# The last modulation of a hybrid trunk layer: from TensorE strips in the state-space stage to GpSimd products in the RWKV stage

## What is computed

```
mod = (silu(cond) @ w_ada + b_ada).reshape(6, 2048)   # cond: 2048 values, w_ada: 2048 x 12288
shift_m, scale_m, gate_m, shift_f, scale_f, gate_f = mod
h = rms_norm(x) * (1 + scale_m) + shift_m
proj = h @ w_in
mixed = concat(ssd_mixer(proj[..., :2592]), rwkv7_mixer(proj[..., 2592:])) @ w_out
x = x + gate_m * mixed
h = rms_norm(x) * (1 + scale_f) + shift_f
x = x + gate_f * expert_choice_ffn(h)                 # 16 experts, 400 MB of weights
y = rms_norm(x)
```

## Time and profile before

| | |
|---|---|
| median of 3 runs | 2311.43 us (2304.68 to 2314.29) |
| the profiled execution | 2312.1 us |
| its span, first to last instruction | 2310.1 us |
| mean granted TensorE clock | 0.978 |
| state-space pairs, from the first of their strips | 197 to 460 us |
| RWKV stage | 461.8 to 1182 us |
| output projection | 1187 to about 1300 us |
| experts | to the end |

### The profile page before, as it was taken

How to read it: one execution, slowest core, us unless ns; L and a number is a source line. 1 busy time by engine, 2 the same in 40 slices (tenths; PEclk the granted TensorE clock), 3 DMA queues, 4 the chain that set the end, 5 groups by cost and what they waited for, 6 DMA issues and landing times. The chain is left out here.

```text
span 2310.1 us, 38354 instructions
## 1 busy us (share of the span) xinstructions
PE 2124.0 (92%) x16411; PEld 1067.5 (46%) x16411; DVE 837.7 (36%) x1839; ACT 402.2 (17%) x810; POOL 157.3 (7%) x186
## 2 busy tenths in 40 slices
PE   6899999899999999999999799899988998899886
PEld 2355555456666666666665433233322432243222
DVE  2244443534566666666431212122222221222113
ACT  2122221222233233323111110001000100010002
POOL 0000111101111101100101000000000000000000
PEclk9999999999999999999999899999999999999998
DMA  9956999832111121211225399999999999999996
GB/s 383 356 184 207 340 349 345 286 87 70 42 50 43 44 52 40 52 34 50 56 77 168 149 368 413 413 413 413 413 413 414 412 413 412 413 412 413 413 413 257
DMA packets 270321, 594.00 MB, mean 257 GB/s; under 512 B 24893, under 2 KB 165463, under 8 KB 249047
## 3 DMA queue, kind: packets, MB, share of 16 engines
q1 hardware_dynamic: 252759, 524.61, 61.0%
q0 software_dynamic: 17408, 67.11, 7.5%
HBM read 586.86 MB, written 4.82 MB: 256 GB/s over the span
## 5 line engine op out<-in xcount | busy, mean ns | idle before, releaser
L2050 PE MATMUL bank<-w_early,picked 128*64 128x512 f32 x1024 | 244.8, 623 | 43.9 <-DMA w_early<-exp_w_up 41.8
L1231 PE MATMUL bank<-arena,w_rkv 128*128 128x384 f32 x736 | 271.7, 502 | 4.4 <-ACT raw_rkv L1468 4.4
L2229 DVE TENSOR_TENSOR x_sum<-x_sum,bank 128x512 f32<-128x512 f32 x180 | 115.5, 684 | 319.9 <-PE bank L2030 319.9
L2074 PE MATMUL bank<-arena,hid 128*64 128x512 f32 x768 | 174.9, 604 | 13.1 <-issue 11.3
L2050 PE MATMUL bank<-arena,picked 128*64 128x512 f32 x768 | 175.4, 598 | 3.8 <-DMA arena<-exp_w_up 3.3
L1231 PEld LDWEIGHTS bank<-arena,w_rkv 128*128 128x128 f32 x736 | 130.1, 189 | 89.7 <-issue 17.4
L2050 PEld LDWEIGHTS bank<-w_early,picked 128*64 128x64 f32 x1024 | 78.2, 142 | 201.7 <-issue 201.3
L832 PE MATMUL bank<-arena,w_xz 128*128 128x384 f32 x448 | 155.3, 494 | 0.4 <-DMA w_xz<-w_in 0.4
L2116 ACT COPY gu<-bank 112x512 f32<-112x512 f32 x32 | 17.2, 589 | 660.8 <-PE bank L2050 660.8
L1203 POOL TENSOR_TENSOR WI<-WX,cst 128x384 f32<-128x384 f32 x80 | 81.1, 1028 | 592.1 <-DVE WX L1673 385.2
L832 PEld LDWEIGHTS bank<-arena,w_xz 128*128 128x128 f32 x448 | 81.6, 190 | 78.3 <-issue 29.3
(11 more groups left out here) (417 smaller groups left out, 2722.5 us busy)
## 6 DMA issues: line engine op xcount, KB each, us to landing
arena<-exp_w_down SPq DMA_DIRECT2D x96, 1024.0 KB, 18.8
w_ada<-w_ada POOLq DMA_DIRECT2D x64, 1024.0 KB, 8.5
w_early<-exp_w_gate SPq DMA_DIRECT2D x64, 1024.0 KB, 18.4
w_early<-exp_w_up SPq DMA_DIRECT2D x64, 1024.0 KB, 18.6
arena<-exp_w_gate SPq DMA_DIRECT2D x48, 1024.0 KB, 18.8
arena<-exp_w_up SPq DMA_DIRECT2D x48, 1024.0 KB, 18.7
w_ada<-w_ada SPq DMA_DIRECT2D x32, 1024.0 KB, 11.3
w_exp<-exp_w_down SPq DMA_DIRECT2D x32, 1024.0 KB, 23.6
```

What stands on the lines that cost most here:

```text
L1231: mm = pe.matmul(ps[feed_bank(i)][:, 0:T], spare[:, n] if first else w[:, m % 3, n % 8], hT[:, n % KC], start=(n % KC == 0), stop=(n % KC ...
L2050: mm = pe.matmul(ps[b][COLS[j], :], picked[:, k, at:at + 64], halves[j][:, c * 1024 + b * 512:c * 1024 + (b + 1) * 512], start=(k == 0), s ...
L2074: mm = pe.matmul(ps[4 + b][COLS[j], :], hid[:, f], wd[:, n * 512:(n + 1) * 512], start=(f == 0), stop=(f == 7))
L2229: V.tensor_tensor(y, y if e else x, ps[(LAST_BANKS[i // 2 % 4] if e == LAST else 6) + i % 2][:], ALU.add).then_inc(S("added"), 1)
```

## The change

Pairs 6 and 7 of the state-space stage have no strips any more, no transposes of them and no `modT` adds. Modulation 5 moves to the RWKV stage. For each of its 8 pairs POOL sums 256 columns of gate_f for both conditions: for each of the 16 blocks of 128 rows it multiplies 128x256 weights (broadcast over the two conditions, so 128x512 values out) by the condition's column, and adds it to `late`. The weights arrive in tiles of two blocks, 256 KB, through two slots, loaded from POOL's own queue. Block 0 follows the mask product of level 3, direction 0; block 1 level 3, direction 1; block 2 level 4, direction 1; block 3 level 5, direction 0; blocks 4 to 15 follow the last mask product. PE sums `late` over the partitions by four matmuls with a column of ones (`reduce_late`) inside the next pair's `gate`, into spare columns of bank 7; ACT adds the bias into `modT` (`late_columns`) between its copies of `wls` and `g`. The last pair's reduction stands in PE's tail, in front of `tail(1, ...)`. `late` and `fo` lie in the unused end of `spare`. POOL's block 0 waits until PE has reduced the pair before.

```diff
+STRIP_PAIRS = 6
...
+LATE = D // PAIRS
...
-            with pool.Fori(1, PAIRS) as c:
+            with pool.Fori(1, STRIP_PAIRS) as c:
                 for n in range(SLOTS_A):
                     pool.wait_ge(S("adah_used"), c * SLOTS_A + (n - AR + 1))
                     load(c, n)
...
-            with eng.Fori(HG, PAIRS - 1) as c:
+            with eng.Fori(HG, STRIP_PAIRS) as c:
                 body(1, c, True)
-            body(1, PAIRS - 1, False)
+            for c in range(STRIP_PAIRS, PAIRS):
+                body(1, c, c + 1 < PAIRS, False)
...
                 def strips(n):
+                    if not ada:
+                        return
...
-                pe.wait_ge(S("adah_row"), c + 1)
-                for i in range(4):
-                    mm = pe.transpose(ps[4][:, i * P:(i + 1) * P], arow[:, i * P:(i + 1) * P], C("ident"))
-                mm.then_inc(S("adah_T"), 1)
+                if ada:
...
+        late_w = sb(st, "late_w", [P, 2, 2, LATE])
+        late = spare[:].rearrange("p k c -> p (k c)")[:, 3 * T:3 * T + 2 * LATE].rearrange("p (a n) -> p a n", a=2)
+        late_t = sb(st, "late_t", [P, 2, LATE])
...
+        LATE_AT = ((0, 1), (1, 2), (2, 2), (2, 3), (3, 4), (4, KC))
...
+            def load_late(p, q):
+                at = 5 * D + p * LATE
+                nc.gpsimd.dma_start(late_w[:, q % 2], w_ada[:, 2 * q:2 * q + 2, at:at + LATE]).then_inc(late_loaded[q % 2], 16)
+
+            def sum_late(p, k0, k1):
+                for k in range(k0, k1):
+                    q = k // 2
+                    if k % 2 == 0:
+                        pool.wait_ge(late_loaded[q % 2], (4 * p + q // 2 + 1) * 16)
+                    if k == 0 and p:
+                        pool.wait_ge(S("late_in"), p)
+                    if k:
+                        pool.wait_ge(S("late_sum"), KC * p + k)
+                    block = late_w[:, q % 2, k % 2].unsqueeze(1).to_broadcast([P, 2, LATE])
+                    ins = nc.gpsimd.tensor_tensor(late_t[:] if k else late, block, cond[:, k, 0:2].unsqueeze(2).to_broadcast([P, 2, LATE]), ALU.mult)
+                    if k:
+                        ins.then_inc(S("late_part"), 1)
+                        pool.wait_ge(S("late_part"), (KC - 1) * p + k)
+                        ins = nc.gpsimd.tensor_tensor(late, late, late_t[:], ALU.add)
+                    ins.then_inc(S("late_sum"), 1)
+                    if k % 2:
+                        pool.wait_ge(S("late_sum"), KC * p + k + 1)
+                        if q + 2 < KC // 2:
+                            load_late(p, q + 2)
+                        elif p + 1 < PAIRS:
+                            load_late(p + 1, q + 2 - KC // 2)
...
                         nc.gpsimd.tensor_tensor(CT[d], W2[d][:, :, 2], m, ALU.mult).then_inc(S(f"CT_ready{d}"), 1)
+                        if n >= 3:
+                            sum_late(p, *LATE_AT[2 * (n - 3) + d])
...
+            def reduce_late(p):
+                pe.wait_ge(S("late_sum"), KC * (p + 1))
+                for b in range(LATE // P):
+                    for a in range(2):
+                        at = LATE_COL + 4 * b + 2 * a
+                        mm = pe.matmul(ps[7][:, at:at + 2], late[:, a, b * P:(b + 1) * P], C("ones")[:, 0:2], start=True, stop=True)
+                mm.then_inc(S("late_in"), 1)
...
             tail(0, 13, 15)
+            pe.wait_ge(S("var_read"), PAIRS)
+            reduce_late(PAIRS - 1)
             tail(1, 8, 15)
             tail(2, 8, 15)
...
+            def late_columns(p):
+                act.wait_ge(S("late_in"), p + 1)
+                for b in range(LATE // P):
+                    at = 5 * KC + p * (LATE // P) + b
+                    src = ps[7][:, LATE_COL + 4 * b:LATE_COL + 4 * b + 4].rearrange("p (a two) -> p a two", a=2)[:, :, 0]
+                    nc.scalar.activation(modT[:, at, :], src, ACT.Identity, bias=par[:, at:at + 1])
```

More of the change, by code:

```diff
@@ L160, in program @@
             reuse_semaphores()
-            rwkv(**env, hT=hT, mixed=mixed, lora=lora, spare=w_narrow)
+            rwkv(**env, cond=cond, hT=hT, mixed=mixed, lora=lora, spare=w_narrow)
         reuse_semaphores()
@@ L834, in feed, with body @@
                         mm.then_inc(S(("x_proj", "z_proj")[j]), 1)
-            def body(g, c, more):
+            def body(g, c, more, ada=True):
                 def fed(n0, n1):
@@ L890, in body @@
                 mm.then_inc(S("yo_in"), 1)
-                pe.wait_ge(S("adah_row"), c + 1)
-                for i in range(4):
-                    mm = pe.transpose(ps[4][:, i * P:(i + 1) * P], arow[:, i * P:(i + 1) * P], C("ident"))
-                mm.then_inc(S("adah_T"), 1)
+                if ada:
+                    pe.wait_ge(S("adah_row"), c + 1)
+                    for i in range(4):
+                        mm = pe.transpose(ps[4][:, i * P:(i + 1) * P], arow[:, i * P:(i + 1) * P], C("ident"))
+                    mm.then_inc(S("adah_T"), 1)
                 fed(FEED[5], 2 * KC)
@@ L920, in body @@
                 nc.scalar.copy(sT[:], ps[2][:].rearrange("p (k n) -> p k n", k=4)).then_inc(S("sT_out"), 1)
-                act.wait_ge(S("adah_used"), c * SLOTS_A + SLOTS_A)
-                nc.scalar.copy(arow[:], ps[4][:]).then_inc(S("adah_row"), 1)
+                if ada:
+                    act.wait_ge(S("adah_used"), c * SLOTS_A + SLOTS_A)
+                    nc.scalar.copy(arow[:], ps[4][:]).then_inc(S("adah_row"), 1)
             turns(act, body)
@@ L928, in _, with body @@
         def _(dve):
-            def body(g, c, more):
-                link = Link(dve, S("ssd_dve"), c * STEPS)
+            def body(g, c, more, ada=True):
+                link = Link(dve, S("ssd_dve"), c * STEPS if ada else STRIP_PAIRS + c * (STEPS - 1))
                 dve.wait_ge(S("x_in_conv"), c + 1)
@@ L1019, with rwkv @@
 TAIL = 3
+LATE = D // PAIRS
 def tail_weights(rows):
     return [rows[:, n * D + 1024:(n + 1) * D].rearrange("p (k c) -> p k c", c=P) for n in range(TAIL)]
-def rwkv(nc, I, O, table, S, sb, ps, cst, par, modT, gain, xT, C, hT, mixed, lora, spare):
+def rwkv(nc, I, O, table, S, sb, ps, cst, par, modT, gain, xT, C, cond, hT, mixed, lora, spare):
     w_in = I["w_in"].rearrange("l (k p) n -> p (l k) n", p=P)
@@ L1069, in rwkv @@
         fin = sb(st, "fin_r", [Q, 2, P])
-        fo = sb(st, "fo", [P, 2, HD])
         M1 = [sb(st, f"M1_{d}", [P, NCH, 3, Q]) for d in range(2)]
@@ L1084, in rwkv @@
         norm_scalar, norm_tensor, norm_vector = ssd_norm(nc, S, ps, par, C, mixed, (t0, rk), (yc, rstd))
+        late_w = sb(st, "late_w", [P, 2, 2, LATE])
+        late = spare[:].rearrange("p k c -> p (k c)")[:, 3 * T:3 * T + 2 * LATE].rearrange("p (a n) -> p a n", a=2)
+        late_t = sb(st, "late_t", [P, 2, LATE])
+        fo = spare[:].rearrange("p k c -> p (k c)")[:, 3 * T + 2 * LATE:3 * T + 2 * LATE + 2 * HD].rearrange("p (d n) -> p d n", d=2)
+        late_loaded = [S(f"late_loaded{n}") for n in range(2)]
         block = st.enter_context(nc.Block())
         HP = (slice(0, Q), slice(Q, P))
+        LATE_COL = T + 64
+        LATE_AT = ((0, 1), (1, 2), (2, 2), (2, 3), (3, 4), (4, KC))
         XX_PARTS = ((0, 4), (4, NCH))
@@ L1194, in _ @@
             ins.then_inc(S("rwkv_fixed"), 1)
+            w_ada = I["w_ada"].rearrange("l (k p) n -> p (l k) n", p=P)
+            def load_late(p, q):
[23 more added lines that the diff above has]
+                            load_late(p + 1, q + 2 - KC // 2)
+            for q in range(2):
+                load_late(0, q)
             for p in range(PAIRS):
@@ L1265, in gate @@
                     pe.matmul(ps[7][0:Q, at:at + 2 * NCH], C("ident")[:, h * Q:(h + 1) * Q], wl[:], start=True, stop=True)
+                if p:
+                    reduce_late(p - 1)
                 small(7, lw[:, 2], lora[:, 2], None, stop=False)
@@ L1528, in body @@
                         nc.scalar.copy(wls[:].rearrange("p h c -> p (h c)"), ps[7][0:Q, T:T + 4 * NCH])
+                        if prev:
+                            late_columns(p - 1)
                         nc.scalar.copy(g[:], ps[7][:, 0:T]).then_inc(S("g_out"), 1)
@@ L1561, in _ @@
             root(PAIRS - 1)
+            late_columns(PAIRS - 1)
         @block.vector
```

15 lines of the change are left out of this document (8 added, 7 removed).

## The result

| | before | after |
|---|---|---|
| median | 2311.69 us (4 runs, 2304.68 to 2314.29) | 2364.1 us (4 runs, 2357.64 to 2369.66) |
| the profiled execution, its span | 2312.1, 2310.1 us | 2369.66, 2368.0 us |

The ratio is 1.0231, 95% interval 1.0215 to 1.0246: the change costs 53 us. The forecast was 2377, in a range of 2316 to 2430.

What follows compares the result with a forecast made beforehand. PE was taken to bound the full state-space pair and the RWKV pairs, DMA the experts. Profiled 2312.1 - 10.5 (state-space) + 71 (seven RWKV pairs at 10.2) + 4 (last pair) = 2377 us, range 2316 to 2430.

Steps and rivals of the forecast that it cites:

- State-space pairs, -10.5: Pairs 6 and 7 without strips: 8.0 and 0.5 off in pair 6, some 3 in pair 7, 1 lost to PE's clock.
- One meeting, 0.71: Delay of a DVE instruction with two SBUF inputs, or SBUF to SBUF, that meets a GpSimd instruction: 0.71 us.
- Scan and subtract at level 4, 1.4: DVE's scan and subtract before the second X update of level 4: two delays of 0.71, 1.4 us a pair.
- kk, 0.1: DVE's clamp and normalisation of kk before level 5's update: 1.4 less 1.3 of idle time, 0.1 us a pair.
- rk and ka, 1.4: DVE's rk and ka before the last X update, for which PE comes at once: 1.4 us a pair.
- The hats, 5.3: Eight DVE products making the next pair's hats, with state rounds queued behind: 8 x 0.71 - 0.4 = 5.3 us a pair.
- Identity and mask steps of the next pair, 1.2: Four DVE steps at the next pair's start, GpSimd still there for about half: 2 x 0.71 - 0.2 = 1.2 us.
- PE's reduction, 0.8: Eight added passes of the column reduction on PE at 0.1 us each: 0.8 us a pair.
- the third rival: Loads are late and hold up GpSimd's mask products and PE: some 9 us a pair more, 2447 us; chance 0.08.
- GpSimd's instructions, 1.34 each: Each 128x512 product or addition in an RWKV pair takes 1.28 us plus 0.06 to start: 1.34 us.
- Last pair, +4: Last RWKV pair: PE waits 2.9 us for GpSimd's last sum before the tail's reduction, plus 0.8: +4 us.
- The first rival: GpSimd loses nearly each meeting and pays, DVE's chain stays: 2318 us in all, not slower; chance 0.13.

Runs made afterwards that it cites:

- the placed kernel: The changed kernel with all of GpSimd's late blocks placed by waits where DVE reads PSUM or idles, and PE's reduction moved ahead of level 1: 2338.26 us, ratio 1.0111.

## Why the prediction was right, and where it was not

The mechanism, the direction and the class of instructions hold; the sum came to 2377 against a profiled 2369.66, the longest of four executions with a median of 2364.1. Its errors partly cancel: the seven RWKV periods came out 15 under their term, the state-space pairs 1.4, the last pair 3.8 and the rest 3.4 over.

- **State-space pairs, -10.5:** -9.15. Pair 6 gave 9.1 (8.5 predicted). Pair 7 gave 0.1 of the 3 (0.7 in the kernel without any late work): with nothing but DVE's results to work on, PE's granted clock is 0.62 there, and its 24 products from M and xq take 0.43 us each instead of 0.28. In the same window of the kernel before the clock was 0.85; the 0.81 of the earlier trace rows belongs to a stretch that reaches 2.4 us past the pair. Strips that run while PE would stand were free, and the clock was higher with them: pair 7 was counted wrong.
- **One meeting, 0.71:** 0.96 beside an unbroken chain of additions, 0.74 beside broadcast products. The step scaled the one delayed scale of the earlier trace rows by length. There DVE arrived 0.54 us into a mask product (877.20 against 876.66); in the chain of additions it arrives each time 0.37 us into one (477.60 against 477.23), with more of it left. The Trainium skill's rule in the section named above, that the loser waits for the whole instruction, would have given up to 1.26 for it.
- **Scan and subtract at level 4, 1.4:** 2.4 to 2.7, for the reason in the placed kernel: GpSimd's mask product and the block's product ran on without a gap. No term priced a meeting with two instructions.
- **kk, 0.1, and the clock, not priced at all:** from the second X update of level 4 to the first of level 5 the two kinds of pair lose 1.5 and 3.05 more. DVE has ended kk 2.3 and 3.9 us ahead of that update, so the update waits for PE and not for kk. PE's granted clock is 0.76 and 0.61 in this stretch, behind its stand, and in the whole pair PE is busy 1.55 and 4.8 us longer for the same passes. That step is missing from the sum.
- **rk and ka, 1.4:** 0.6 and 2.3. In the longer kind 1.6 more are lost from there to the mask on XX, at a granted clock of 0.77.
- **The hats, 5.3:** 0.75 and 0.7 in the one kind of pair; in the other 2.1 at the first four, of which 0.9 comes back by y. This is the term that failed most. Each of the eight was charged a meeting; in the trace one run of four in each of these two pairs went through, and GpSimd paid. In the kernel with the waits between mask products, seven of eight did meet in the pair from 712.29: there they cost 6.7 us by y, more than the term.
- **Identity and mask steps of the next pair, 1.2:** nothing. The bulk of the pair from 711.87 ends at 789.94, 78.1 us after its start (84 predicted), and GpSimd then idles 6.2 us before the next mask product. It is not the bound, as predicted.
- **PE's reduction, 0.8:** 0.9. **ACT's columns, loads:** nothing that shows; a load landed 3.2 us after its issue (median of 64), so the third rival had no ground.
- **GpSimd's instructions, 1.34 each:** the broadcast product took 1.04, not 1.28, and the addition 1.27; with waits they average 1.10 and 1.47.
- **Last pair, +4:** PE's wait for the last sum was 2.46 (2.9 predicted) and the reduction 1.02, but the pair grew by 7.8, of which 4.7 are there without any product (87.83 against 83.14). It holds two reductions, that of the pair before and its own (16 passes more), and PE is busy 80.90 us there instead of 77.34, at a granted clock of 0.98 instead of 1.00; the rest of the 4.7 was not taken apart.

Per pair the terms gave 10.2; measured is 8.0 in the mean (55.9 / 7), 6.8 in the shorter kind and 11.7 in the longer. That the sum of a pair lies between them is in part luck: hats counted some 4 too high stand against a clock that was not counted. Of the signs to look for, the period (85 to 92), the untouched evictions, the stands of PE ahead of state rounds and the wait in the tail came; "the hats about twice as long" did not (816 against 543 ns in the mean of all, from 546 to 1190 by product), nor did a pair 7 shorter by 2 to 3. One sign of being wrong came as well: the form with a broadcast factor took 1.04 and not 1.28.

The first rival, that GpSimd pays and not DVE, is true of single runs of hats, but DVE's 90 us more of busy time rule it out for the whole.

## What to carry to other kernels

An engine's idle time is not free room: before moving work onto GpSimd, list the other engine's instructions of the same stretch by where their operands lie, and place GpSimd's work beside those that read PSUM or stand idle; the same arithmetic cost 53 us unplaced and 3 placed. Read a saving pair by pair before paying for it: half of what was moved had been hidden already, and leaving that half where it was hidden, which also halves what the RWKV pairs pay, made the version that wins. A freed engine can run slower: in pair 7 PE's granted clock was 0.84 and 0.85 with strips in its waits, and 0.62 and 0.69 without.

## What was not expected of the hardware

- GpSimd instructions without a wait between them kept DVE out through the whole run: a half shift of v took 3.78 us instead of 0.48, from 738.35 to past two mask products and a block's product (738.89 to 741.84). With a wait of some 0.06 us between the two mask products and behind them the same instruction fell to 474 ns in the mean, and the smaller half ahead of it took 1113 instead of 352.
- A DVE scale from SBUF to SBUF is held up even by memsets (0.64 us instead of 0.36), which do not touch the two-input forms. A DVE reciprocal from SBUF to SBUF is not held up by GpSimd's products and additions (2.55 us, four of four).
- After a stand of 3.0 to 3.3 us PE's granted clock fell to between 0.50 and 0.89 in the windows of five us with it and behind it. After one of 1.9 us, at the same place of the program, it fell to 0.71 in one pair and stayed at 1.00 in another (the kernel with the waits between mask products). So one slow scan on DVE cost a pair more than its own delay, and not always the same.
